# One group of attention and chunk work per slot between the projections of a hybrid decoder layer

## The chip, the cores and the metric

The kernel runs on one core of a Trainium2 chip. The metric is the time of one execution on the device in microseconds. The head loop, which the change touches, is four iterations of the same program.

## The reference, cut to what matters

One layer: a projection of the modulated input h feeds stick-breaking attention (8 heads of 64) and a chunkwise mLSTM (4 heads of 128); both are gated, projected, merged and normed. SEQ and D_MODEL are 1024.

```python
proj = h @ w_in + b_in
...
z = jnp.einsum('bhtd,bhsd->bhts', qb, kb).astype(jnp.float32) * scale
log_beta = jax.nn.log_sigmoid(z)
log_rem = jnp.where(causal, jax.nn.log_sigmoid(-z), 0.0)
suffix = lax.cumsum(log_rem, axis=3, reverse=True) - log_rem
attn = jnp.where(causal, jnp.exp(log_beta + suffix), 0.0)
outs.append(jnp.einsum('bhts,bhsd->bhtd', attn.astype(vb.dtype), vb))
...
qk = jax.nn.silu(causal_depthwise_conv(jnp.concatenate([ml_q, ml_k], -1), conv_w, conv_b))
...
num = (w_inter[..., None] * jnp.einsum('bhtd,bhde->bhte', qb, C)
       + jnp.einsum('bhts,bhse->bhte', s_mat, vb))
...
x = LayerNorm(alpha * x + (1 + gate) * y)
```

## The kernel before, in words

All engines run programs written out by hand; the only order is that of each engine's queue, and semaphores hold them together. Each iteration of the head loop (`iteration`, one per engine) handles one mLSTM head and one pair of attention heads whose q, k, v were projected in the iteration before. Its backbone on TensorE is `project` (L618): nine jobs of 48 matmuls, each 128x128 by 128x512, in which every product is split into three terms (high by high, low by high, high by low). These 432 matmuls are counted through; the number n of a matmul is the clock by which everything else is placed. A job fills two banks (`proj_ps`), one per half of the sequence; ScalarE copies each out behind its 24th matmul (`evac` in `events`, L153) and VectorE and ScalarE split the weights loaded by SP into high and low (`split`). The `tasks` between two values of n are what ScalarE and VectorE do of these.

The attention is cut into NS = 12 slots (`SLOTS`): a block of 128 queries against 1 to 4 blocks of 128 keys (1, 2, 3, 4, 1, 4, 2, 4, 3, 4, 4, 4 blocks). Per slot and for both heads h of the pair: `scores` on TensorE (L716: three products on 64 rows of the array, head 0 in rows 0 to 63, head 1 in rows 64 to 127, into `z_ps[h]`), `odds` on ScalarE (exponential, L998), `cap_odds` on VectorE (L1472), `remainders` on ScalarE (L1007), `stick_left` on VectorE (a scan, L1486), `weights_of` on GpSimd (product, L568), `turn_weights` on TensorE (transposes of the weights back into `z_ps[h]`, L734), `turned` on ScalarE (copy to `at_sb[h]`, L1020) and `weighted_values` on TensorE (L744: 64 columns of the array per head, both heads side by side).

The mLSTM needs a convolution first, over m_k and m_q: `conv_sum` in four halves (L1538, VectorE), `conv_exps` and `conv_sigmoid` on ScalarE with `conv_bound` between them, and `conv_silu` (product, L1556). m_k, v and the mLSTM's v are transposed by `mlstm_third` (L787). From slot 4 on there is one chunk per slot: `mlstm_first` (L763: scores of the chunk, new state, query by state), `chunk_scores` on VectorE (L1578), `mlstm_second` (L780: scores by values), `chunk_values` (L1592); after the last one `norm_head` (L1611).

A slot interrupts the projections twice. At its start TensorE runs `mlstm_first(s)`, `weighted_values(s - 2)` and `scores(s)`; after 13 or 16 projection matmuls it runs `turn_weights(s - 1)`, `mlstm_second(s)` and `mlstm_third(s)`; 14 or 16 more follow. `segments` (L133) has the numbers; `tail` (L147) has those behind slot 11, where the last two slots' values and the last transposes stand alone. ScalarE and VectorE follow the same four marks p0 to p3 of a slot. In this text a slot is one of the twelve, and a group is what TensorE runs between two stretches of projections.

## Time and profile before

| | us |
|---|---|
| median of 3 runs | 979.25 (978.87 to 979.35) |
| profiled execution | 978.75 |
| its span | 977.0 |
| TensorE busy | 942.3 |
| VectorE busy | 599.7 |
| ScalarE busy | 454.5 |
| GpSimd busy | 167.0 |

The mean granted clock of TensorE over the span is 0.997 of full speed. In a timeline the times are microseconds from the span's start; a matmul's length overlaps the next one's, so the distance from start to start is what one costs. A matmul of float32 data (not the split ones) stands as two records, a transpose as one. An entry "x8" is eight records in a row. What stands in brackets is idle time and what ended it.

### The profile page before, as it was taken

Reading aid. Unit: us, or ns where it says so; the run is one execution under the profiler, and the core shown is the slowest. Engines: PE = TensorE matmul, PEld = TensorE weight load, DVE = VectorE, ACT = ScalarE, POOL = GpSimd, SP = SyncE. Lnnn points to the kernel's source line nnn. Section 1 sums busy time; section 2 is a strip of 40 time slices with the busy share of each in tenths; the row PEclk is TensorE's granted clock in tenths of the full one; section 3 lists DMA queues with packets and bytes.
Section 4 is the critical chain, followed back from the end, with each engine's and each line's share of the span. In section 5 each row is a group of like instructions: output and inputs, shape, how many; then the busy total and the mean of one; then the engine's idle time right before and its main releaser. Section 6 shows DMA issues by size and latency. Waiting matters only on the chain.

```text
span 977.0 us, 13097 instructions
## 1 busy us (share of the span) xinstructions
PE 942.3 (96%) x4965; PEld 757.3 (78%) x4965; DVE 599.7 (61%) x1144; ACT 454.5 (47%) x813; POOL 167.0 (17%) x138
## 2 busy tenths in 40 slices
PE   2999999999999999999999999999999999999996
PEld 1677778888778888778888778788888888878885
DVE  4857785666775757866657857543653333345986
ACT  2454575553665544665644756433843222242100
POOL 1010122240132430123220233211100000001200
PEclk9999999999999999999999999999999999999998
DMA  9932211102201012111113101115721222215232
GB/s 231 291 91 55 70 28 44 33 23 69 72 24 54 22 44 85 35 44 34 39 27 98 44 22 45 33 47 189 245 59 43 65 55 52 89 44 182 90 127 86
DMA packets 99561, 73.96 MB, mean 76 GB/s; under 512 B 4616, under 2 KB 90760, under 8 KB 99500
## 3 DMA queue, kind: packets, MB, share of 16 engines
q1 hardware_dynamic: 94828, 58.44, 22.2%
q0 software_dynamic: 2368, 8.41, 2.6%
q10 hardware_dynamic: 2304, 6.29, 1.7%
q8 instruction: 39, 0.64, 0.3%
q14 instruction: 22, 0.18, 0.1%
HBM read 64.59 MB, written 8.40 MB: 75 GB/s over the span
## 4 chain that ended last, share of the span: by engine, by line
PE 82%; DVE 10%; DMA 3%; SPq 2%; ACT 2%; issue 1%; DVEq 0%; ACTq 0%
PE bank L636 41%; PE bank L616 9%; PE bank L615 9%; PE bank L614 9%; PE bank L757 4%; PE bank L741 3%; DMA a_raw<-in_w_ada 2%; PE bank L730 2%; DVE m_q L1547 2%; DVE wL L1344 1%; PE bank L770 1%; SPq L453 1%; DVE m_q L1559 1%; PE bank L713 1%; PE bank L731 1%
## 5 line engine op out<-in xcount | busy, mean ns | idle before, releaser
L636 PE MATMUL bank<-hH,wH 128*128 128x512 f32 x688 | 274.8, 399 | 0.6 <-DVE wL L1344 0.6
L636 PE MATMUL bank<-hL,wH 128*128 128x512 f32 x688 | 272.9, 397 | 0.0
L636 PE MATMUL bank<-hH,wL 128*128 128x512 f32 x688 | 269.1, 391 | 0.0
L574 POOL TENSOR_TENSOR ez<-ez,rem 128x512 f32<-128x512 f32 (+3 forms) x96 | 136.0, 1436 | 411.1 <-DVE rem L1496 411.1
L636 PEld LDWEIGHTS bank<-hH,wH 128*128 128x128 f32 x688 | 129.1, 188 | 38.4 <-issue 10.7
L1344 DVE SCALAR_TENSOR_TENSOR wL<-w_raw,wH 128x512 fp32r<-128x512 f32 x116 | 87.6, 759 | 113.8 <-ACT wH L916 113.3
L636 PEld LDWEIGHTS bank<-hH,wL 128*128 128x128 f32 x688 | 129.4, 188 | 26.6
L636 PEld LDWEIGHTS bank<-hL,wH 128*128 128x128 f32 x688 | 129.4, 188 | 24.6 <-issue 1.0
L916 ACT ACTIVATE wH<-w_raw 128x512 fp32r<-128x512 f32 x116 | 72.5, 627 | 98.0 <-PE bank L616 71.1
L1496 DVE TENSOR_TENSOR_SCAN rem<-rem,ones 128x512 f32<-128x512 f32 (+3 forms) x96 | 88.6, 964 | 38.7 <-ACT rem L1018 38.7
L1005 ACT ACTIVATE ez<-bank 128x512 f32<-128x512 f32 (+3 forms) x96 | 41.9, 489 | 95.1 <-PE bank L732 95.1
L1480 DVE TENSOR_SCALAR ez<-ez 128x512 f32<-128x512 f32 (+3 forms) x80 | 27.5, 344 | 53.7 <-ACT ez L1005 52.7
L614 PE MATMUL bank<-hH,yH 128*128 128x512 f32 x128 | 51.1, 400 | 0.0
L603 POOL TENSOR_TENSOR yL<-yT,yH 128x1024 fp32r<-128x1024 f32 x6 | 14.4, 2398 | 214.5 <-ACT yH L1273 214.5
L616 PE MATMUL bank<-hH,yL 128*128 128x512 f32 x128 | 50.7, 396 | 0.0
L615 PE MATMUL bank<-hL,yH 128*128 128x512 f32 x128 | 50.7, 396 | 0.0
L1014 ACT ACTIVATE rem<-ez 128x512 f32<-128x512 f32 (+3 forms) x96 | 44.9, 517 | 7.2 <-DVE ez L1483 7.1
L1018 ACT ACTIVATE rem<-rem 128x512 f32<-128x512 f32 (+3 forms) x96 | 44.4, 510 | 0.0
L1026 ACT ACTIVATE at<-bank 128x512 f32<-128x512 f32 (+3 forms) x96 | 41.3, 483 | 5.6 <-PE bank L741 5.6
L615 PE MATMUL bank<-hL,wH 128*128 128x512 f32 x112 | 43.7, 390 | 0.0
L614 PE MATMUL bank<-hH,wH 128*128 128x512 f32 x112 | 43.7, 390 | 0.0
L616 PE MATMUL bank<-hH,wL 128*128 128x512 f32 x112 | 43.6, 389 | 0.0
(238 smaller groups left out, 1513.7 us busy)
## 6 DMA issues: line engine op xcount, KB each, us to landing
w_raw<-in_w_in SPq DMA_DIRECT2D x104, 256.0 KB, 2.9
a_raw<-in_w_ada SPq DMA_DIRECT2D x16, 512.0 KB, 7.4
x_rows<-in_x SPq DMA_DIRECT2D x8, 512.0 KB, 6.5
raw<-in_w_ada POOLq DMA_DIRECT2D x8, 512.0 KB, 4.6
x_in<-in_x SPq DMA_DIRECT2D x8, 512.0 KB, 4.2
out_y<-res SPq DMA_DIRECT2D x7, 512.0 KB, 2.9
raw<-in_w_out SPq DMA_DIRECT2D x10, 256.0 KB, 4.8
m_w<-bm_scratch ACTq DMA_DIRECT2D x4, 512.0 KB, 3.9
```

Source lines behind the costliest of these rows:

```text
L574: g.tensor_tensor(e, e, r, ALU.mult).then_inc(a_done[h], 1)
L614: t.matmul(ps, aH, bH, start=k == 0, stop=False)
L615: t.matmul(ps, aH, bL, start=False, stop=False)
L616: return t.matmul(ps, aL, bH, start=False, stop=k == kt - 1)
L636: ins = t.matmul(banks(number)[half][:], w, a, start=(r == 0), stop=(r == JOB_MM // 2 - 1))
L916: a.activation(wH[:, slot, :, 0:width], w_raw[:, slot, :, 0:width], ACT.Copy, scale=scale)\
L1005: a.activation(ez[s % 2][h][:, 0:w], z_ps[h][:, 0:w], ACT.Exp).then_inc(ex_done[h], 1)
L1014: a.activation(rem[s % 2][h][:, 0:w], ez[s % 2][h][:, 0:w], ACT.Ln, bias=1.0).then_inc(ln_done[h], 1)
L1018: a.activation(r, r, ACT.Exp, scale=-1.0).then_inc(rem_done[h], 1)
L1026: a.activation(at_sb[h][:, 0:w], z_ps[h][:, 0:w], ACT.Copy).then_inc(at_out[h], 1)
L1344: v.scalar_tensor_tensor(out=wL[:, slot, :, 0:width], in0=w_raw[:, slot, :, 0:width], scalar=scale, in1=wH[:, slot, :, 0:width], op0=ALU.m ...
L1496: v.tensor_tensor_scan(back, back, ones[:, 0:1].to_broadcast((P, w)), first, ALU.mult, ALU.min)\
```

## The change

On TensorE one group per slot takes the place of the two: group g runs `turn_weights(g - 2)`, `weighted_values(g - 3)`, `mlstm_second(g)` (now for the chunk of slot g - 1), `mlstm_first(g)`, `scores(g)` and `mlstm_third(g)`, then a whole stretch of projections (`GROUPS`: group 0 at n = 48, then 83, 118, 148 and every 26). Groups 12 and 13 hold only what is left over of the turned weights, values and the last chunk; the values of slot 11 stand at the iteration's end. The turned weights of head 0 go to a bank of their own (`misc_ps[2]`), those of head 1 to `z_ps[1]`, ahead of the same group's scores of head 1, which wait for ScalarE's copy of them. `at_sb` has two buffers.

ScalarE copies the turned weights at the start of a slot (`turned(s - 2)`, head 1 first). The convolution's steps stand earlier: the third and fourth sums in slots 0 and 1 (were 1 and 2), the product for m_k in slot 1 (was 2), exponential, bound, sigmoid and product for m_q in slot 2 (were 3). `m_tmp` is made with the chunk's scores; `chunk_values` runs one slot later, ahead of `chunk_scores`, and waits for three fills of its bank. `gate_y(0)` and `store_y(0)` stand one slot later, `norm_head` behind the chunk values of group 12. `place0` to `place2` of ScalarE and VectorE are dissolved into the iterations.

```diff
@@ -130,24 +130,17 @@
-def segments():
-    at, out = PRE, []
-    for s in range(NS):
-        sizes = (8, 8, 16) if s < 3 else (7, 6, 14)
-        row = [at]
-        for n in sizes:
-            at += n
-            row.append(at)
-        out.append(row)
-    return out, JOB_MM * NJ
-def tail():
-    at = segments()[0][-1][-1]
-    return [at, at + (JOB_MM * NJ - at) // 2, JOB_MM * NJ]
+GROUPS = [PRE, 83, 118] + [148 + 26 * n for n in range(NS - 1)]
+JOBS_END = JOB_MM * 9
+def stretch(g):
+    lo, hi = (GROUPS + [JOBS_END])[g:g + 2]
+    return lo, lo + (hi - lo) // 4, lo + (hi - lo) // 2, hi
...
@@ -254,7 +247,7 @@
         rem = [[it(f"rem{b}{h}", [P, HALF]) for h in range(2)] for b in range(2)]
-        at_sb = [it(f"at{h}", [P, HALF]) for h in range(2)]
+        at_sb = [[it(f"at{b}{h}", [P, HALF]) for h in range(2)] for b in range(2)]
         y_stage = it("y_stage", [P, HALF])
...
@@ -390,6 +383,8 @@
             return i * 2 * NJ + (2 * PRO_JOBS + c_)
+        turned_ps = [misc_ps[2], z_ps[1]]
         def banks(number):
...
@@ -718,14 +713,15 @@
                 tt, kk = slice(tb * P, (tb + 1) * P), slice(lo, hi)
+                if s == 0:
+                    pe.wait_ge(pair_split, i * 4 + 4)
                 for h in range(2):
                     r = slice(64 * h, 64 * h + 64)
-                    if s > 1:
-                        pe.wait_ge(at_out[h], i * NS + s - 1)
-                    elif s > 0:
+                    if h and s != 1:
+                        if i or s:
+                            pe.wait_ge(at_out[h], i * NS + max(s - 1, 0))
+                    elif i or s:
                         pe.wait_ge(ex_done[h], i * NS + s)
-                    elif h == 0:
-                        pe.wait_ge(pair_split, i * 4 + 4)
                     ps = z_ps[h][:, 0:hi - lo]
...
@@ -733,12 +729,19 @@
             def turn_weights(i, s):
-                for h in range(2):
-                    if s + 1 < NS:
+                for h in (1, 0):
+                    if h and s < NS - 1:
                         pe.wait_ge(ex_done[h], i * NS + s + 2)
+                    elif h:
+                        pe.wait_ge(at_out[h], i * NS + s)
+                    elif i or s:
+                        pe.wait_ge(at_out[h], i * NS + s)
+                    else:
+                        pe.wait_ge(dec_drained, 1)
                     pe.wait_ge(a_done[h], i * NS + s + 1)
                     for b in range(n_keys(s) // P):
-                        ins = t.transpose(z_ps[h][:, b * P:(b + 1) * P], ez[s % 2][h][:, b * P:(b + 1) * P], ident[:])
+                        ins = t.transpose(turned_ps[h][:, b * P:(b + 1) * P], ez[s % 2][h][:, b * P:(b + 1) * P],
+                                          ident[:])
                     ins.then_inc(at_filled[h], 1)
...
@@ -755,7 +758,7 @@
                         ins = t.matmul(y_ps[64 * h:64 * h + 64, tt], v_tok[:, j, 64 * h:64 * h + 64],
-                                       at_sb[h][:, b * P:(b + 1) * P], start=b == 0 and not continues(s),
+                                       at_sb[s % 2][h][:, b * P:(b + 1) * P], start=b == 0 and not continues(s),
                                        stop=b == n - 1 and closes(s), skip_group_check=True)
...
@@ -766,7 +769,7 @@
                         pe.wait_ge(conv_done, i * 2 + 2)
-                    pe.wait_ge(m_drained[0], m_count(0, i, F_CHUNK + 2 * cc))
+                    pe.wait_ge(m_drained[0], m_count(0, i, F_CHUNK + 2 * cc) - (1 if cc else 0))
                     t.matmul(misc_ps[0][:, 0:P], m_k[:, tt], m_q[:, tt], start=True, stop=True)\
...
@@ -778,8 +781,8 @@
             def mlstm_second(i, s):
-                if s >= 4:
-                    cc = s - 4
+                if s >= 5:
+                    cc = s - 5
                     pe.wait_ge(m_drained[0], m_count(0, i, F_CHUNK + 2 * cc) + 1)
...
@@ -805,25 +808,20 @@
             def iteration(i, last):
-                segs, _ = segments()
                 project(i, 0, PRE)
-                for s in range(NS):
-                    start, _, middle, end = segs[s]
-                    mlstm_first(i, s)
-                    if s > 1:
-                        weighted_values(i, s - 2)
-                    scores(i, s)
-                    project(i, start, middle)
-                    if s > 0:
-                        turn_weights(i, s - 1)
-                    mlstm_second(i, s)
-                    mlstm_third(i, s)
-                    project(i, middle, end)
-                weighted_values(i, NS - 2)
-                ends = tail()
-                project(i, ends[0], ends[1])
-                turn_weights(i, NS - 1)
-                project(i, ends[1], ends[2])
+                for g in range(NS + 2):
+                    if g >= 2:
+                        turn_weights(i, g - 2)
+                    if g >= 3:
+                        weighted_values(i, g - 3)
+                    if g <= NS:
+                        mlstm_second(i, g)
+                    if g < NS:
+                        mlstm_first(i, g)
+                        scores(i, g)
+                        mlstm_third(i, g)
+                    lo, _, _, hi = stretch(g)
+                    project(i, lo, hi)
                 weighted_values(i, NS - 1)
...
@@ -1000,8 +998,6 @@
                     act.wait_ge(z_done[h], i * NS + s + 1)
-                    if s > 1:
-                        act.wait_ge(at_filled[h], i * NS + s - 1)
                     a.activation(ez[s % 2][h][:, 0:w], z_ps[h][:, 0:w], ACT.Exp).then_inc(ex_done[h], 1)
...
@@ -1017,13 +1013,14 @@
                     a.activation(r, r, ACT.Exp, scale=-1.0).then_inc(rem_done[h], 1)
-            def turned(i, s, h):
+            def turned(i, s):
                 w = n_keys(s)
-                act.wait_ge(at_filled[h], i * NS + s + 1)
-                if s > 0:
-                    act.wait_ge(pv_done[h], i * NS + s)
-                a.activation(at_sb[h][:, 0:w], z_ps[h][:, 0:w], ACT.Copy).then_inc(at_out[h], 1)
+                for h in (1, 0):
+                    act.wait_ge(at_filled[h], i * NS + s + 1)
+                    if i * NS + s > 1:
+                        act.wait_ge(pv_done[h], i * NS + s - 1)
+                    a.activation(at_sb[s % 2][h][:, 0:w], turned_ps[h][:, 0:w], ACT.Copy).then_inc(at_out[h], 1)
             def store_y(i, tc):
...
@@ -1137,23 +1130,7 @@
-            def place1(i, s):
...
             def iteration(i, last):
-                segs, _ = segments()
...
@@ -1161,31 +1138,40 @@
                 for s in range(NS):
-                    p0, p1, p2, p3 = segs[s]
+                    p0, p1, p2, p3 = stretch(s)
+                    if s >= 2:
+                        turned(i, s - 2)
                     odds(i, s)
+                    if s == 2:
+                        conv_exps(i, 1)
                     if s == 3:
-                        conv_exps(i, 1)
+                        token_major(i, F_MV, m_vtok)
                     tasks(i, p0, p1, last)
-                    place0(i, s)
                     remainders(i, s)
-                    if s == 3:
+                    if s == 0:
+                        load_forget_row(i)
+                        token_major(i, F_V, v_tok)
+                    if s == 2:
                         conv_sigmoid(i, 1)
+                    if s == 7:
+                        store_y(i, 0)
                     tasks(i, p1, p2, last)
-                    if s > 0:
-                        turned(i, s - 1, 0)
-                        turned(i, s - 1, 1)
-                    place1(i, s)
-                    place2(i, s)
+                    if s == 0:
+                        conv_exps(i, 0)
+                    if s == 2:
+                        act.wait_ge(w_sum, i + 1)
+                        a.activation(m_w[:], m_w[:], ACT.Exp).then_inc(w_exp, 1)
                     tasks(i, p2, p3, last)
-                ends = tail()
-                tasks(i, ends[0], ends[1], last)
-                turned(i, NS - 1, 0)
-                turned(i, NS - 1, 1)
+                    if s == 0:
+                        conv_sigmoid(i, 0)
+                turned(i, NS - 2)
                 act.wait_ge(var_done, i + 1)
                 a.activation(small[:, 24:32], small[:, 16:24], ACT.Ln, bias=EPS).then_inc(rstd_ln, 1)
                 act.wait_ge(rstd_ln, i + 1)
                 a.activation(small[:, 24:32], small[:, 24:32], ACT.Exp, scale=-0.5).then_inc(rstd_exp, 1)
-                tasks(i, ends[1], ends[2], last)
+                tasks(i, GROUPS[NS], GROUPS[NS + 1], last)
+                turned(i, NS - 1)
+                tasks(i, GROUPS[NS + 1], JOBS_END, last)
                 store_y(i, 1)
...
@@ -1584,15 +1570,15 @@
                     .then_inc(m_drained[1], 1)
-            def aggregate(cc):
-                link.mark(v.bn_aggr(mv[:, cc], stat[:, cc]))
-            def chunk_values(i, cc):
-                dve.wait_ge(m_filled[0], m_count(0, i, F_CHUNK + 2 * cc) + 2)
                 v.tensor_scalar(m_tmp[:], misc_ps[1][:, 2 * P:3 * P + 1], h_tok[:, 1, cc:cc + 1], None, ALU.mult)\
                     .then_inc(m_drained[1], 1)
+            def aggregate(cc):
+                link.mark(v.bn_aggr(mv[:, cc], stat[:, cc]))
+            def chunk_values(i, cc):
+                dve.wait_ge(m_filled[0], m_count(0, i, F_CHUNK + 2 * cc) + (2 if cc == NC - 1 else 3))
                 dve.wait_ge(m_drained[1], m_count(1, i, F_CHUNK + 2 * cc) + 2)
...
@@ -1637,28 +1623,7 @@
-            def place0(i, s):
...
             def iteration(i, last):
-                segs, end = segments()
...
@@ -1666,27 +1631,37 @@
                 for s in range(NS):
-                    p0, p1, p2, p3 = segs[s]
-                    place0(i, s)
+                    p0, p1, p2, p3 = stretch(s)
+                    if s >= 5:
+                        chunk_values(i, s - 5)
+                    if s >= 4:
+                        chunk_scores(i, s - 4)
                     cap_odds(i, s)
+                    if s == 1:
+                        conv_silu(i, 0)
                     if s == 2:
-                        conv_silu(i, 0)
-                    if s == 3:
                         conv_bound(i, 1)
-                    if s == 5:
+                    if s == 6:
                         gate_y(i, 0)
                     tasks(i, p0, p1, last)
                     stick_left(i, s)
-                    if s == 3:
+                    tasks(i, p1, p2, last)
+                    if s == 0:
+                        conv_sum(i, 1)
+                        pair_gate(i)
+                        conv_bound(i, 0)
+                    if s == 1:
+                        chunk_weights(i)
+                        conv_sum(i, 3)
+                    if s == 2:
+                        weighted_keys(i)
                         conv_silu(i, 1)
-                    if s >= 4:
-                        chunk_values(i, s - 4)
-                    tasks(i, p1, p2, last)
-                    place1(i, s)
-                    place2(i, s)
                     tasks(i, p2, p3, last)
+                    if s == 0:
+                        conv_sum(i, 2)
+                chunk_values(i, NC - 1)
                 norm_head(i)
-                tasks(i, segs[-1][3], end, last)
+                tasks(i, GROUPS[NS], JOBS_END, last)
                 gate_y(i, 1)
```

## Rows read from the trace of the kernel before

**Rows 1.** The page's part 1, and the longest piece of the chain that ended last.
```profile
PE 942.3 (96%) x4965; PEld 757.3 (78%) x4965; DVE 599.7 (61%) x1144; ACT 454.5 (47%) x813; POOL 167.0 (17%) x138
...
667.12 43.55 PE bank L636 x192
```

**Rows 2.** By line: TensorE's idle time before L713 and L770 (us, times).
```profile
  DVE m_k L1559: 2.5, 4
...
L770 PE MATMUL bank<-m_q,m_k 128*128 128x128 f32 x64 | 12.8, 281 | 2.9 <-DVE m_q L1559 2.9
```

**Rows 3.** Timeline of TensorE, second iteration: start, length (us), what, idle before.
```profile
267.49 0.60 PE L741 MATMUL bank<-ident,ez 128*128 128x128 f32 x4
268.72 1.06 PE L713 MATMUL bank<-ident,m_k 128*128 128x128 f32 x8 [0.63 <-DVE m_k L1559]
...
282.45 0.39 PE L636 MATMUL bank<-hH,wL 128*128 128x512 f32 x1
283.55 0.49 PE L770 MATMUL bank<-m_q,m_k 128*128 128x128 f32 x2 [0.71 <-DVE m_q L1559]
```

**Rows 4.** Timeline of TensorE, slots 4 and 5 of the same iteration.
```profile
288.79 1.03 PE L741 MATMUL bank<-ident,ez 128*128 128x128 f32 x8
289.66 0.39 PE L784 MATMUL bank<-m_vtok,m_s 128*128 128x129 f32 x2
289.81 0.48 PE L636 MATMUL bank<-hL,wH 128*128 128x512 f32 x1
...
293.10 0.38 PE L770 MATMUL bank<-m_q,m_k 128*128 128x128 f32 x2
...
293.54 0.39 PE L777 MATMUL bank<-m_state,m_q 128*128 128x129 f32 x2
293.86 1.09 PE L757 MATMUL bank<-at,v_tok 128*64 128x128 f32 x16
294.88 0.51 PE L730 MATMUL bank<-kH,qH 64*128 64x512 f32 x2
295.22 0.41 PE L731 MATMUL bank<-kL,qH 64*128 64x512 f32 x2
...
295.79 0.50 PE L636 MATMUL bank<-hH,wH 128*128 128x512 f32 x1
```

**Rows 5.** Timeline of TensorE: scores behind projections, transposes behind values.
```profile
254.00 0.39 PE L636 MATMUL bank<-hL,wH 128*128 128x512 f32 x1
254.32 0.39 PE L730 MATMUL bank<-kH,qH 64*128 64x256 f32 x2
...
374.04 1.09 PE L713 MATMUL bank<-ident,m_num 128*128 128x128 f32 x8
374.89 0.47 PE L636 MATMUL bank<-hH,wH 128*128 128x512 f32 x1
```

**Rows 6.** Timeline of VectorE, slots 0 to 2.
```profile
252.11 1.22 DVE L1535 TENSOR_TENSOR g_cur<-next_g,sig 128x1024 f32<-128x1024 f32 x1
...
257.75 1.27 DVE L1496 TENSOR_TENSOR_SCAN rem<-rem,ones 128x256 f32<-128x256 f32 x2 [0.23 <-ACT rem L1018]
...
260.74 0.68 DVE L1554 TENSOR_SCALAR m_num<-m_num 128x1024 f32<-128x1024 f32 x1
...
263.73 0.54 DVE L1545 TENSOR_SCALAR m_q<-conv_in,h_col 128x512 f32<-128x512 f32 x1
...
266.55 0.29 DVE L1480 TENSOR_SCALAR ez<-ez 128x256 f32<-128x256 f32 x1
```

**Rows 7.** Timeline of ScalarE, slots 2 and 3.
```profile
267.07 0.94 ACT L1014 ACTIVATE rem<-ez 128x384 f32<-128x384 f32 x2 [0.50 <-DVE ez L1483]
...
274.06 0.62 ACT L916 ACTIVATE wH<-w_raw 128x512 fp32r<-128x512 f32 x1
...
279.38 1.04 ACT L1119 ACTIVATE sig<-sig 128x1024 f32<-128x1024 f32 x1
...
281.42 0.85 ACT L1026 ACTIVATE at<-bank 128x384 f32<-128x384 f32 x2
```

More of the change, by code:

```diff
@@ L1127, in token_major @@
                                  ACT.Copy).then_inc(m_drained[n], 1)
-            def place0(i, s):
-                if s == 6:
-                    store_y(i, 0)
             def load_forget_row(i):
@@ L1138, in load_forget_row @@
                 act.dma_start(m_w[:].rearrange("p c t -> p (c t)"), row.broadcast_to((P, S))).then_inc(bm_in, 16)
-            def place1(i, s):
-                if s == 0:
-                    load_forget_row(i)
-                    token_major(i, F_V, v_tok)
-            def place2(i, s):
-                if s == 0:
-                    conv_exps(i, 0)
-                if s == 1:
-                    conv_sigmoid(i, 0)
-                    act.wait_ge(w_sum, i + 1)
-                    a.activation(m_w[:], m_w[:], ACT.Exp).then_inc(w_exp, 1)
-                if s == 3:
-                    token_major(i, F_MV, m_vtok)
             def iteration(i, last):
-                segs, _ = segments()
                 act.wait_ge(sig_capped, i * 2 + 1)
@@ L1586, in chunk_scores @@
                     .then_inc(m_drained[1], 1)
+                v.tensor_scalar(m_tmp[:], misc_ps[1][:, 2 * P:3 * P + 1], h_tok[:, 1, cc:cc + 1], None, ALU.mult)\
+                    .then_inc(m_drained[1], 1)
             def aggregate(cc):
@@ L1592, in chunk_values @@
             def chunk_values(i, cc):
-                dve.wait_ge(m_filled[0], m_count(0, i, F_CHUNK + 2 * cc) + 2)
-                v.tensor_scalar(m_tmp[:], misc_ps[1][:, 2 * P:3 * P + 1], h_tok[:, 1, cc:cc + 1], None, ALU.mult)\
-                    .then_inc(m_drained[1], 1)
+                dve.wait_ge(m_filled[0], m_count(0, i, F_CHUNK + 2 * cc) + (2 if cc == NC - 1 else 3))
                 dve.wait_ge(m_drained[1], m_count(1, i, F_CHUNK + 2 * cc) + 2)
@@ L1638, in gate_head @@
                     dve.wait_ge(m_drained[n], m_count(n, i, F_HN) + 1)
-            def place0(i, s):
-                if s >= 4:
-                    chunk_scores(i, s - 4)
-            def place1(i, s):
-                if s == 0:
-                    conv_sum(i, 1)
-                if s == 1:
-                    conv_bound(i, 0)
-            def place2(i, s):
-                if s == 0:
-                    pair_gate(i)
-                if s == 1:
-                    chunk_weights(i)
-                    conv_sum(i, 2)
-                if s == 2:
-                    conv_sum(i, 3)
-                    weighted_keys(i)
             def iteration(i, last):
-                segs, end = segments()
                 split_pair(i)
@@ L1679, in iteration @@
                     stick_left(i, s)
-                    if s == 3:
-                        conv_silu(i, 1)
-                    if s >= 4:
-                        chunk_values(i, s - 4)
-                    tasks(i, p1, p2, last)
-                    place1(i, s)
-                    place2(i, s)
+                    tasks(i, p1, p2, last)
[8 more added lines that the diff above has]
+                        weighted_keys(i)
+                        conv_silu(i, 1)
                     tasks(i, p2, p3, last)
+                    if s == 0:
+                        conv_sum(i, 2)
+                chunk_values(i, NC - 1)
                 norm_head(i)
-                tasks(i, segs[-1][3], end, last)
+                tasks(i, GROUPS[NS], JOBS_END, last)
                 gate_y(i, 1)
```

## The prediction

> **What bounds the kernel now.** The page comes first: TensorE is busy 96% of the span [rows 1]. The other engines matter only where TensorE waits for one of them, or where the change gives TensorE other work or another order. The longest unbroken piece in the chain of waits is 192 projection matmuls in 43.55 us, 0.227 us each [rows 1]; this is the unit below. Next comes the view by line of what TensorE waited for. In the head loop (four iterations) it stops twice per iteration, both times behind the convolution: before the transposes of m_k, 2.5 us in all, four times, and before the first chunk product L770, 2.9 us in all [rows 2]. The timeline gives the whole price. The four transposes at 267.49 need 4 x 0.109 = 0.44 (eight take 289.66 - 288.79 = 0.87 [rows 4]), so the next could start at 267.93 and starts at 268.72: 0.79 lost. The matmul at 282.45 is followed after 1.10, not 0.23: 0.87 lost [rows 3]. That is **1.66 us per iteration, 6.6 us in four**.
>
> **What an interruption costs.** The middle one (transposes, second chunk product): the last chunk product lasts 289.81 - 289.66 = 0.15 where it otherwise takes 0.22, and the 14 projections behind it take 3.29 where 14 x 0.227 = 3.18: net 0.03 to 0.04 us [rows 4]. So stopping the projections for full-array work is nearly free. The other interruption costs more, because its matmuls use half of the array: values are 64 columns wide, scores 64 rows. Entering values adds 0.10 (293.54 to 293.86 is 0.32; two chunk products in front take 0.44, so 0.22 each) [rows 4]. Entering scores from a full-array matmul adds the same: 254.00 to 254.32, 0.32 instead of 0.227 [rows 5]. Leaving values for full-array transposes costs the first transposes: eight of them last 0.85, while 7 x 0.109 plus the 0.03 that remains of a last one before a projection is 0.79: 0.06 more [rows 5]. What counts is changes of shape, not interruptions.
> The Trainium skill (TensorEngine Tiling (Array Packing), Key Properties) says that changing the tiling mode drains the engine. The rows agree, with about 0.1 us each; the page gives no price, and its rule speaks against this change.
>
> **Part by part, per iteration.**
> (a) *Group order on TensorE.* Middle interruptions go: one of V transposes, eleven of turned weights, one in the tail, 13 x 0.03 = -0.4.
> (b) *Shapes.* Before, values pass straight into scores ten times. After, the chunk products stand between them from slot 4 on, and slot 2 has scores without values. Entries into scores from full-array work rise from 2 to 11: +9 x 0.09 = +0.8. Exits from values into full-array work other than a projection rise from 1 to 10: +9 x 0.06 = +0.5. The number of entries into values stays 12. The trace has no chunk product right behind values, so the 0.06 is taken from transposes there; bounds 0 and 0.1. Sum of (b) **+1.3**, bounds +0.8 and +1.8.
> (c) *Convolution moved up.* Both stalls go, -1.66: the product for m_k would end near 258.7, transposes of m_k come near 264.9; the product for m_q ends near 276, the first chunk product comes after 283. What is late next is (d).
> (d) *A new wait between the two heads' scores.* The turned weights of head 1 now go into the bank that head 1's scores of the same group need. ScalarE must copy them out in between. Behind that wait on TensorE stand head 1's scores, transposes and all projections of the stretch. From group 4 on there is cover: from the end of head 1's transposes to the scores lie values, chunk products and head 0's transposes, 1.6 us and more, against two copies of 0.85 in all [rows 7] and an idle ScalarE. Groups 2 and 3 have no chunk products.
> Group 2: TensorE reaches it at 267.49 less ten matmuls (2.3), scores of slot 2 (0.8), values (0.45) and transposes (0.2) = 263.7. Head 1's block is turned at 264.0, copied by 264.25; its scores could start at 264.0. Cost **0.3**.
> Group 3: the copy stands behind all of slot 2 on ScalarE, which in turn waits for VectorE's last convolution sum. VectorE: pair gate until 253.3 [rows 6], then the cap (0.6), sum 2.8, caps of slot 1 0.8, m_k product 1.2, split 0.65, scan 1.2, split 0.65, chunk weights 2.4 and sum 2.85, with a few tenths while GpSimd works beside it: the sum ends at 266.7. (Lengths: 266.55 - 263.73 = 2.82 for a sum; 263.73 - 260.74 = 2.99 for cap and chunk weights; scan 1.27 [rows 6]; the product over 1024 columns as the pair gate, 1.2.) ScalarE from 266.75: exponential 1.0, bias copy 0.6, logarithm and exponential of slot 2 2 x 0.84, the sigmoid's two steps 2.04, split 0.55, exponential of m_w 1.0, bias copy 0.6, split 0.55, head 1's copy 0.35 (281.42 - 279.38 = 2.04; 0.94 for two 384-wide ones that overlap by 0.1; a split 0.62 less the overlap of what follows, a bias copy the same [rows 7]): 8.3, so 275.0. TensorE: 263.7 + 0.2 + scores 1.1 + transposes 0.85 + 30 x 0.227 + 0.1 = 272.7 at group 3; turned weights 0.45 and values 0.45 bring it to 273.6. The six score products of both heads run as pairs, 295.79 - 294.88 = 0.91 [rows 4]. Head 1's start at 275.0 and take the 0.9 alone: cost **1.4**. A VectorE chain faster by 1 us makes it 0.4, one slower by 0.8 makes it 2.2. Sum of (d) **+1.7**, bounds +0.5 and +2.6.
> In program order head 0's three products stand ahead of head 1's. The rows show both first products starting together and then both second ones, 0.34 later [rows 4]. The Trainium skill (TensorE: Matmul & The Clock Gate, Part 3) says matmuls start strictly in program order; by that the second head would start 0.7 later anyhow and (d) would be 0.7 smaller in group 3. The row decides against it.
> (e) *Edits at nothing.* Second buffer for turned weights: its wait is a slot old. m_tmp computed with the chunk scores, chunk values a slot later: VectorE moves 0.3 us of work inside a slot in which it idles. The wait for three fills instead of two holds VectorE's caps behind the first chunk product for some 0.5 us; GpSimd's product has two slots until it is turned, where it had one and a half. The store of y on ScalarE's queue goes one slot later, behind nothing that is needed before the next half. The forget row is issued right after slot 0's remainders, at 248.3 to 248.6 as now, with over 10 us until it is read. SP's loads follow VectorE's splits: the split for matmul 108 is ready near 259.3, needed at 261.4. Head norm: chunk values end some 3.3 us after matmul 382, ScalarE waits for the variance ahead of the bias copy of 384, which ends about 6 us after 382; the bank is wanted at 408, 8 us after. The head's result is wanted 16 us after 382 and is there after 9. Without that cover each microsecond late costs one.
>
> **The sum.** -1.66 - 0.4 + 1.3 + 1.7 = +0.94 per iteration, times 4 = **+3.8 us**. The profiled execution took 978.75 (span 977.0 and 1.75 around it), so 982.5; it stands 0.5 under the median of 979.25, which gives 983.0. I put 982.8.
>
> **Rivals.**
> A, *the new wait is short* (slot 2's chain on ScalarE ends before 274): (d) is 0.6, the sum -0.2 per iteration: 978.5. Against it stands 8.3 us of work on ScalarE that can't start before the last sum. For it, my VectorE chain has ten terms and each may be a tenth too long.
> B, *the shapes cost nothing more and the wait is short*: -1.66 - 0.4 + 0.4 to 0.8 per iteration, 972.5 to 974. For it: no row shows chunk products between values and scores. Against it: entries of 0.1 in every slot, from either kind.
> C, *slower by a lot*: the wait between the heads is unmet in later groups too. It decides where ScalarE is still in its previous tasks when a group begins, by more than the cover of 1.6 us. A bias copy or sigmoid pair due at the end of a stretch (matmul 168 before 174, 384 behind the variance) would do that. Each such slot costs up to 1 us; three per iteration on top of my sum are +12: 995; one is 987. Against it: the last due task lies 6 to 26 matmuls ahead of the group.
> D, *the change doesn't do what it says*, and the chunk product still waits for the convolution: not less than 0.9 per iteration back, 986.4. Seven microseconds of slack speak against it.
>
> **How the numbers follow.** My forecast (981.2 to 986) 0.5; A 0.2; B 0.15; C 0.1; D 0.05. The range takes A, D and the nearer part of both B and C: 976.5 to 987. About 0.2% (2 us) is what a measurement of this kernel can tell from no change. Faster by more than that: B, 0.15 and a little of A, 0.17. Same: most of A and the lower end of the forecast, 0.23. Slower: 0.60.
>
> **What would show it.** In the profile after: no idle time of TensorE before L713 and L770 behind the convolution's product (c); projections interrupted 12 times per iteration with scores and at two more places (a); 0.09 more at each chunk product that leads into scores, with 0.06 at the first behind values (b); in group 3 a gap of 1 to 2 us before head 1's first score product, released by ScalarE's copy of turned weights, and three score products of head 0 alone in front of it (d). If that gap is missing A or B holds. If such gaps are there in groups 4 to 11, C does. A gap before matmul 408 or at the transposes of m_num would say that (e) was wrong about the head norm.

## The result and the profile after

The changed kernel takes **989.0 us** (median, 988.7 to 990.7) against 979.3: a ratio of 1.0105, interval 1.0093 to 1.0117, 9.7 us slower. Forecast were 982.8 us and a range up to 987.0: the direction was right, the size was not. The profiled execution has a span of 987.1 us, 10.1 longer than before.

The page of the changed kernel, part 1 and the engines of the chain that ended last (projections are now L631, values L760, turned weights L743, scores L726 to L728, chunk products L773 to L780 and L787, plain transposes L708):

```profile
span 987.1 us, 13064 instructions
...
PE 954.4 (97%) x4965; PEld 766.4 (78%) x4965; DVE 605.6 (61%) x1144; ACT 456.1 (46%) x813; POOL 165.6 (17%) x138
...
PE 91%; DMA 3%; SPq 2%; DVE 2%; ACT 2%; issue 1%; DVEq 0%; ACTq 0%
```

TensorE is busier than before [rows 1] by 12 us, with the same 4965 records. It makes up 91% of the chain that ended last. Both old stops are gone: no idle time is left before L708 or L773 behind the convolution's product, where the stops had cost 0.79 and 0.87 us per iteration [rows 2, 3]. What came instead stands in group 3. The timeline of TensorE in the second iteration (start, length, what, idle before it):

```profile
274.49 0.60 PE L743 MATMUL bank<-ident,ez 128*128 128x128 f32 x4
275.02 0.44 PE L760 MATMUL bank<-at,v_tok 128*64 128x128 f32 x4
275.39 0.50 PE L726 MATMUL bank<-kH,qH 64*128 64x512 f32 x1
275.73 0.39 PE L727 MATMUL bank<-kL,qH 64*128 64x512 f32 x1
275.96 0.39 PE L728 MATMUL bank<-kH,qL 64*128 64x512 f32 x1
277.39 0.49 PE L726 MATMUL bank<-kH,qH 64*128 64x512 f32 x1 [1.04 <-ACT at L1023]
...
278.28 1.73 PE L708 MATMUL bank<-ident,m_vraw 128*128 128x128 f32 x8
279.66 0.78 PE L631 MATMUL bank<-hL,wH 128*128 128x512 f32 x1
280.23 0.63 PE L631 MATMUL bank<-hH,wL 128*128 128x512 f32 x1
280.66 0.63 PE L631 MATMUL bank<-hH,wH 128*128 128x512 f32 x1
...
282.43 0.39 PE L631 MATMUL bank<-hH,wL 128*128 128x512 f32 x1
282.66 0.40 PE L631 MATMUL bank<-hH,wH 128*128 128x512 f32 x1
```

Head 0's three score products start at 275.39, 275.73 and 275.96. Head 1's first starts only at 277.39, 2.00 us behind head 0's, where both start together in [rows 4]. All four iterations have it; the view of waits (total us, times, longest) names ScalarE's copy of the turned weights for both the weight load and the matmul:

```profile
PEld bank L726 <- ACT at L1023: 5.9, 4, 1.5
...
PE bank L726 <- ACT at L1023: 4.2, 4, 1.1
```

The last lines of the timeline show a second loss. From 280.23 to 280.66 a projection takes 0.43 us; from 282.43 to 282.66 it takes 0.23. The view by stretches gives, for each stretch, the busy time of TensorE, its weight loads, VectorE, ScalarE and GpSimd, then TensorE's granted clock as a share of full speed, the DMA share and GB/s:

```profile
132.20:136.90 4.70, 3.64 (x23) 2.35 (x22) 4.05 (x6) 4.42 (x10) 1.26 (x2) 1.00 0.24 56
274.50:278.60 4.10, 3.06 (x18) 1.83 (x17) 3.54 (x5) 3.82 (x9) 1.17 (x2) 1.00 0.27 63
278.60:282.00 3.40, 3.40 (x14) 2.92 (x12) 1.49 (x5) 2.94 (x6) 0.00 (x0) 0.50 0.30 78
282.00:286.70 4.70, 4.70 (x22) 3.87 (x21) 2.34 (x2) 1.41 (x3) 3.17 (x2) 1.00 0.00 0
...
421.90:425.30 3.40, 3.40 (x14) 2.76 (x13) 2.05 (x6) 2.30 (x6) 0.00 (x0) 0.51 0.46 119
```

From 278.6 to 282.0 the granted clock is 0.50 of full speed, 1.2 GHz instead of 2.4, and again from 421.9. Before each of the two, TensorE had stood idle for 1.04 and 1.05 us; the lower clock began 1.2 and 0.7 us after that idle time ended. The same wait in iterations 1 and 4 (1.06 us each, ending at 135.2 and 565.0) was not followed by it. An iteration lasts 143.84 and 143.77 us in the two that have it, from transposes of m_num to transposes of m_num; it was 140.5.

That two of four iterations have the lower clock belongs to this one execution. Of the four executions of the changed kernel, the slowest (990.7 us) has a mean granted clock of 0.993 and a span 1.7 us longer than the profiled one, as one more such stretch would give. Only one execution was traced, so this is inferred.

Each chunk group from slot 4 on is also longer. Group 5:

```profile
295.46 1.04 PE L743 MATMUL bank<-ident,ez 128*128 128x128 f32 x8
296.43 0.88 PE L760 MATMUL bank<-at,v_tok 128*64 128x128 f32 x12
297.23 0.49 PE L787 MATMUL bank<-m_vtok,m_s 128*128 128x129 f32 x2
297.56 0.39 PE L773 MATMUL bank<-m_q,m_k 128*128 128x128 f32 x2
...
298.00 0.39 PE L780 MATMUL bank<-m_state,m_q 128*128 128x129 f32 x2
298.32 0.51 PE L726 MATMUL bank<-kH,qH 64*128 64x512 f32 x2
```

The first chunk product behind values, L787, takes 297.56 - 297.23 = 0.33 instead of 0.22, and the last one ahead of scores 298.32 - 298.00 = 0.32 instead of 0.22: 0.10 and 0.09 more, in eight groups per iteration.

### The profile page after: what moved, and what is told of

The parts are those of the page before. It is cut to its first block, busy times and chain, and to the rows that moved or that the text cites. A ratio compares the mean times of both kernels' runs of the same rounds, so it can differ in the third digit from the quotient of the medians.

```text
span 987.1 us, 13064 instructions
## 1 busy us (share of the span) xinstructions
PE 954.4 (97%) x4965; PEld 766.4 (78%) x4965; DVE 605.6 (61%) x1144; ACT 456.1 (46%) x813; POOL 165.6 (17%) x138
## 4 chain that ended last, share of the span: by engine, by line
PE 91%; DMA 3%; SPq 2%; DVE 2%; ACT 2%; issue 1%; DVEq 0%; ACTq 0%
PE bank L631 47%; PE bank L611 9%; PE bank L610 9%; PE bank L609 9%; PE bank L760 4%; PE bank L743 3%; DMA a_raw<-in_w_ada 2%; PE bank L726 2%; PE bank L708 2%; PE bank L787 1%; PE bank L727 1%; PE bank L728 1%; SPq L448 1%; PE bank L773 1%; PE bank L778 1%; DVE a_acc L1321 1%
## 5 line engine op out<-in xcount | busy, mean ns | idle before, releaser
L631 PE MATMUL bank<-hH,wH 128*128 128x512 f32 x688 | 271.4, 395 | 0.7 <-DVE wL L1330 0.7
L631 PE MATMUL bank<-hL,wH 128*128 128x512 f32 x688 | 271.0, 394 | 0.0
L631 PE MATMUL bank<-hH,wL 128*128 128x512 f32 x688 | 270.7, 393 | 0.0
L1330 DVE SCALAR_TENSOR_TENSOR wL<-w_raw,wH 128x512 fp32r<-128x512 f32 x116 | 97.7, 844 | 139.0 <-ACT wH L914 138.4
L631 PEld LDWEIGHTS bank<-hH,wH 128*128 128x128 f32 x688 | 129.6, 188 | 31.2 <-issue 3.8
L631 PEld LDWEIGHTS bank<-hH,wL 128*128 128x128 f32 x688 | 129.7, 188 | 30.6 <-issue 3.9
L631 PEld LDWEIGHTS bank<-hL,wH 128*128 128x128 f32 x688 | 129.9, 189 | 27.8 <-issue 1.5
L609 PE MATMUL bank<-hH,wH 128*128 128x512 f32 x112 | 43.7, 390 | 0.0
L760 PE MATMUL bank<-at,v_tok 128*64 128x128 f32 x576 | 42.0, 281 | 0.0
```

What stands on the lines that cost most here:

```text
L609: t.matmul(ps, aH, bH, start=k == 0, stop=False)
L631: ins = t.matmul(banks(number)[half][:], w, a, start=(r == 0), stop=(r == JOB_MM // 2 - 1))
L760: ins = t.matmul(y_ps[64 * h:64 * h + 64, tt], v_tok[:, j, 64 * h:64 * h + 64], at_sb[s % 2][h][:, b * P:(b + 1) * P], start=b == 0 and no ...
L1330: v.scalar_tensor_tensor(out=wL[:, slot, :, 0:width], in0=w_raw[:, slot, :, 0:width], scalar=scale, in1=wH[:, slot, :, 0:width], op0=ALU.m ...
```

## The experiments

After the result the theory was this sum, in us: stalls gone -6.6; head 1 late in group 3, 2.0 x 4 = +8; in group 2, +1.3; the lower clock +3.1; changes of array shape, net of the saved interruptions, +4.1. Together +9.9, against a span longer by 10.1. The 4.1 is what was left when the other terms had been taken off, not a measured term. The rivals: the time is a property of the whole group; ScalarE and VectorE limit slot 2 whatever their order; the clock is a matter of its own. The kernel before, measured beside the experiments, took 978.9 and 979.0 us; every ratio below is against it.

**copy_first** (on the changed kernel; in ScalarE's iteration, and in VectorE's `weighted_keys` ahead of the split of slot 2):

```diff
-                    if s >= 2:
+                    if s >= 2 and s != 3:
                         turned(i, s - 2)
...
                     if s == 2:
-                        act.wait_ge(w_sum, i + 1)
-                        a.activation(m_w[:], m_w[:], ACT.Exp).then_inc(w_exp, 1)
+                        turned(i, 1)
                     tasks(i, p2, p3, last)
+                    if s == 2:
+                        act.wait_ge(w_sum, i + 1)
+                        a.activation(m_w[:], m_w[:], ACT.Exp).then_inc(w_exp, 1)
...
                     stick_left(i, s)
+                    if s == 2:
+                        weighted_keys(i)
                     tasks(i, p1, p2, last)
...
                     if s == 2:
-                        weighted_keys(i)
                         conv_silu(i, 1)
```

> The changed kernel (989.0 us), with ScalarE's copy of the turned weights of slot 1 moved ahead of the bias copy of matmul 144, the split behind it and the exponential of m_w, and VectorE's weighted keys moved ahead of its split in slot 2. Theory (the wait between the two heads' scores in group 3 costs 2.0 us per iteration, and with it come the two stretches at 1.2 GHz, 3.1 us in all): the idle time before head 1's first score product in group 3 goes, the granted clock stays at its upper level through the head loop, and the time falls by 8 + 3 = 11 us to 978. Rival (ScalarE and VectorE are the limit in slot 2, whatever their order): the wait only moves to the transposes behind the scores, the time stays at 985 to 989. Rival on the clock (the two stretches at the lower clock have nothing to do with this wait): they are still there, and the time is 981.

Measured: **977.8 us**, ratio 0.9989 (0.9980 to 0.9998). Group 3 of the second iteration on TensorE:

```profile
273.19 0.50 PE L726 MATMUL bank<-kH,qH 64*128 64x512 f32 x2
...
274.09 1.08 PE L708 MATMUL bank<-ident,m_vraw 128*128 128x128 f32 x8
```

The scores run as pairs again, 0.90 us for six, and the clock stays at its upper level in the whole head loop. The theory's 978 stands; both rivals fall. The span is 11.3 us shorter than the changed kernel's, more than any other part of the change gives or takes. The edit moves ScalarE's copy ahead of three tasks, and moves VectorE's weighted keys along; what each of the two moves gives by itself was not run.

**order** (on the changed kernel) and **both** (order and copy_first together):

```diff
-                    if g >= 3:
-                        weighted_values(i, g - 3)
                     if g <= NS:
                         mlstm_second(i, g)
                     if g < NS:
                         mlstm_first(i, g)
+                    if g >= 3:
+                        weighted_values(i, g - 3)
+                    if g < NS:
                         scores(i, g)
```

> The changed kernel with the chunk's products moved ahead of the values in each group: turned weights, second and first products, values, scores. No work is added or removed. Theory (a change of array shape costs 0.09 us going into scores and 0.10 us coming out of values, 8 groups per iteration): 0.19 x 8 x 4 = 6 us less, 983. Rival (the products cost what they cost, in any order): 989. The wait of group 3 and its stretches at the lower clock stay in both.

> Both edits together on the changed kernel: the copy of slot 1 first, and the chunk's products ahead of the values. Theory: the two gains add, 989 - 11 - 6 = 972; below the kernel before (979.3) by 7. Rival (the copy is then late for the scores in the groups from 4 on, because less TensorE work lies between): 975 to 980.

Measured: order **982.2 us**, ratio 1.0032 (1.0019 to 1.0044); both **971.8 us**, ratio 0.9927 (0.9912 to 0.9942). The gains add. In `order` the idle time of 1.05 to 1.06 us is still there in all four iterations and two of them have the stretch at the lower clock, this time the first and the third. That gives its price: from transposes of m_num to transposes of m_num the second iteration lasts 140.68 us and the third 142.30, with the same wait in both, so one stretch costs 1.6 us. The executions of `order` fall into two groups: three with a mean clock of 0.994 and a span of 981.1 us, three with 0.996 and 979.4 to 979.7, as with one stretch fewer. The median lies between them. The traced executions of `order` and of the changed kernel have two stretches each, and their spans, 981.1 and 987.1, give the price of the order alone: 6.0 us. Group 5 of `both`:

```profile
288.14 1.04 PE L743 MATMUL bank<-ident,ez 128*128 128x128 f32 x8
289.01 0.39 PE L787 MATMUL bank<-m_vtok,m_s 128*128 128x129 f32 x2
289.24 0.39 PE L773 MATMUL bank<-m_q,m_k 128*128 128x128 f32 x2
...
290.00 0.88 PE L760 MATMUL bank<-at,v_tok 128*64 128x128 f32 x12
```

L787 is back at 289.24 - 289.01 = 0.23. With nothing added or removed the order inside the group is worth 6 us. The rival that products cost the same in any order falls.

**conv_only** (on the kernel before; the convolution's steps stand where the change puts them, except that the sigmoid for m_q comes behind the copy of the turned weights of slot 1; excerpt of VectorE and ScalarE):

```diff
                 if s == 0:
                     pair_gate(i)
+                    conv_bound(i, 0)
                 if s == 1:
                     chunk_weights(i)
-                    conv_sum(i, 2)
+                    conv_sum(i, 3)
                 if s == 2:
-                    conv_sum(i, 3)
                     weighted_keys(i)
+                    conv_silu(i, 1)
...
                     tasks(i, p2, p3, last)
+                    if s == 0:
+                        conv_sum(i, 2)
...
-                if s == 1:
-                    conv_sigmoid(i, 0)
+                if s == 2:
+                    conv_sigmoid(i, 1)
                     act.wait_ge(w_sum, i + 1)
```

> The kernel before with only the convolution's steps moved up by a slot, as in the change; two interruptions per slot as before. Theory (the two stalls of 0.79 and 0.87 us per iteration are all that this part of the change can give): 979.3 - 6.6 = 972.7, no idle time before the transposes of m_k and the first chunk product. Rival (moving the steps delays ScalarE's copies of turned weights, and the stall goes to the scores of slot 3): 976 to 980.

Measured: **971.6 us**, ratio 0.9926 (0.9911 to 0.9941). The transposes of m_k follow the turned weights without a pause:

```profile
265.66 0.60 PE L741 MATMUL bank<-ident,ez 128*128 128x128 f32 x4
266.10 1.04 PE L713 MATMUL bank<-ident,m_k 128*128 128x128 f32 x8
```

266.10 - 265.66 = 0.44 is what four transposes take. The span falls by 7.2 us, 0.6 more than the 6.6 that the rows had given. The kernel before shows where it comes from:

```profile
283.88 0.39 PE L775 MATMUL bank<-m_vtok,m_ktok 128*128 128x129 f32 x2
```

The first chunk product, which follows the second stall, starts at 283.55 [rows 3] and takes 283.88 - 283.55 = 0.33, where it takes 0.21 in conv_only without the idle time. The second stall so cost 0.99 us and both together 1.8 per iteration. This part alone, with two interruptions per slot left as they were, is as fast as the best version of the merged group (971.8).

**extra_stop** (on conv_only):

```diff
                         turn_weights(i, s - 1)
-                    mlstm_second(i, s)
                     mlstm_third(i, s)
-                    project(i, middle, end)
+                    project(i, middle, middle + 3)
+                    mlstm_second(i, s)
+                    project(i, middle + 3, end)
```

> The kernel before with the convolution moved up (971.6 us), and one more interruption per slot from slot 4 on: three projection matmuls stand between the turned weights and the chunk's second product. 32 more interruptions of the projections by full-array work. Theory (such an interruption costs 0.03 us): 971.6 + 1.0 = 972.6. Rival (an interruption costs 0.2 us or more, which is what taking one of two per slot away was to bring): 978 or more.

Measured: **972.7 us**, ratio 0.9934 (0.9922 to 0.9946), 1.1 more than conv_only for 32 more interruptions: 0.03 us each, but the intervals of the two overlap. The profiles say the same: the second iteration goes from 138.71 to 138.91 us, 0.03 for each of eight. The rival's 0.2, which would be 6.4 us, is excluded.

**half_wait** (on the changed kernel; `tasks` gets a filter, true for splits alone):

```diff
                         a.activation(m_w[:], m_w[:], ACT.Exp).then_inc(w_exp, 1)
-                    tasks(i, p2, p3, last)
+                        tasks(i, p2, p3, last, False)
+                        turned(i, 1)
+                        tasks(i, p2, p3, last, True)
+                    else:
+                        tasks(i, p2, p3, last)
```

> The changed kernel (989.0 us) with only the split behind matmul 144 moved behind ScalarE's copy of the turned weights of slot 1; exponential and bias copy stay ahead of it. Theory: the idle time before head 1's scores in group 3 falls from 1.05 to about 0.5 us, 0.52 x 4 = 2.1 less. If the stretches at the lower clock come from the length of that idle time they go too, 989 - 2.1 - 3.1 = 983.8; rival (any wait there brings them, or none does): they stay, 986.9.

Measured: **983.9 us**, ratio 1.0050 (1.0036 to 1.0064). Group 3 of the second iteration:

```profile
275.48 0.39 PE L728 MATMUL bank<-kH,qL 64*128 64x512 f32 x1
276.41 0.49 PE L726 MATMUL bank<-kH,qH 64*128 64x512 f32 x1 [0.54 <-ACT at L1023]
```

The idle time is 0.54 us (0.52 to 0.54 in the four iterations), and the granted clock stays at its upper level through the head loop; the mean clock of all four executions is 0.997 or 0.998. Its second iteration lasts 141.72 us where the changed kernel's lasts 143.84: 2.12 less, of which 0.5 is the shorter wait and 1.6 the clock. So the stretches at 1.2 GHz come with this wait at its full length, and half of it doesn't bring them. Why some iterations have them and others with the same wait don't, these runs don't tell.

**between** (on the kernel before, slots 4 to 11):

```diff
-                    mlstm_first(i, s)
                     if s > 1:
                         weighted_values(i, s - 2)
+                    mlstm_first(i, s)
                     scores(i, s)
```

> The kernel before with one swap in each of the slots 4 to 11: values, then the chunk's first three products, then scores (they stood ahead of the values). Nothing is added. Theory (the changes of array shape cost 0.09 + 0.10 us at each of 32 places, whatever else the change does): 979 + 6.2 = 985. Rival (in the changed kernel it was the group as a whole, not the shapes): 979, no difference.

Measured: **981.4 us**, ratio 1.0023 (1.0014 to 1.0032): 2.4 more, neither 6.2 nor nothing. The expectation forgot that in slot 4 the values, 0.8 us, now stand where TensorE had waited 0.87 for the convolution, and hide that stall: its trace has no idle time before L770. 6.2 - 3.5 = 2.7. The shape itself costs what was said:

```profile
294.30 0.49 PE L770 MATMUL bank<-m_q,m_k 128*128 128x128 f32 x2
294.62 0.39 PE L775 MATMUL bank<-m_vtok,m_ktok 128*128 128x129 f32 x2
```

0.32 for the first product behind values, against 0.22: two of them take 293.54 - 293.10 = 0.44 in [rows 4].

**third_early** (on both; the transposes of m_k of group 2 ahead of the scores):

```diff
                         turn_weights(i, g - 2)
+                    if g == 2:
+                        mlstm_third(i, g)
...
                         scores(i, g)
-                        mlstm_third(i, g)
+                        if g != 2:
+                            mlstm_third(i, g)
```

> The changed kernel with the copy of slot 1 first and the chunk's products ahead of the values (971.8 us), and in group 2 the transposes of m_k moved between the turned weights and the scores, 0.85 us of work while ScalarE copies head 1's block. Theory (in group 2 the scores of the two heads run partly one after the other, 0.3 us, and transposes behind scores cost 0.06): 0.38 x 4 = 1.5 less, 970.3. Rival (scores of slot 2 come 0.85 later and ScalarE's chain of slot 2 with them, so that the wait of group 3 comes back): 972 to 974.

Measured: **972.0 us**, ratio 0.9926 (0.9914 to 0.9939): no gain. Groups 2 and 3 of the second iteration:

```profile
262.17 1.03 PE L708 MATMUL bank<-ident,m_k 128*128 128x128 f32 x8
263.14 0.45 PE L726 MATMUL bank<-kH,qH 64*128 64x384 f32 x2
...
271.70 0.74 PE L726 MATMUL bank<-kH,qH 64*128 64x512 f32 x2
272.04 0.39 PE L727 MATMUL bank<-kL,qH 64*128 64x512 f32 x1
...
272.89 1.06 PE L708 MATMUL bank<-ident,m_vraw 128*128 128x128 f32 x8
```

In group 2 the scores run as pairs from 263.14 on, which wins 0.3 us. The transposes ahead of them take 0.97 instead of 0.85, since they now lead into scores. In group 3 the six score products take 272.89 - 271.70 = 1.19 instead of 0.90: head 1 is late again, by 0.3, though without idle time. Won 0.3, lost 0.1 and 0.3: the rival was right in kind.

## Why the prediction was right or wrong

- **(c), the stalls**: right, a little low. Both are gone. They were worth 1.8 us per iteration, not 1.66: conv_only's span is 7.2 shorter, because the first product behind a stall is slower too.
- **(a), an interruption costs 0.03**: right (extra_stop). The middle interruptions were nearly free; at this price taking them away gives about 1.5 us in all (an estimate: the second iteration's projections are broken 27 times before and 15 after, 12 fewer, where the sum had 13).
- **(b), shapes**: right in kind, a little low. Entering scores +0.09 as forecast; leaving values +0.10 to 0.11 instead of 0.06. That term was read from plain transposes behind values; a chunk product behind values pays more. The net of (a) and (b) was forecast at 3.6 us. It was not measured by itself; copy_first's span leaves 975.8 - 977.0 + 7.2 - 1.3 = 4.7 for it (7.2 for the stalls, 1.3 for group 2). The prices found here would give 9 x 0.09 + 9 x 0.10 - 12 x 0.03 = 1.35 per iteration, 5.4 us; the difference of 0.7 stays open.
The Trainium skill (TensorEngine Tiling (Array Packing), Key Properties) says that a change of tiling mode drains the engine. The runs between, order and both agree with it: each change costs about 0.1 us.
- **(d), head 1's wait**: right in mechanism and place, but 0.6 us too short in group 3, 2.4 us in four iterations. Group 2 cost 0.32, as said; its timeline shows head 1's first product 0.33 behind head 0's:

```profile
265.68 0.44 PE L726 MATMUL bank<-kH,qH 64*128 64x384 f32 x1
265.96 0.34 PE L727 MATMUL bank<-kL,qH 64*128 64x384 f32 x1
266.01 0.44 PE L726 MATMUL bank<-kH,qH 64*128 64x384 f32 x1
266.14 0.33 PE L728 MATMUL bank<-kH,qL 64*128 64x384 f32 x1
...
266.73 1.09 PE L708 MATMUL bank<-ident,m_k 128*128 128x128 f32 x8
```

Group 3 cost 2.0 where the sum had 1.4 and its bound 2.2. ScalarE, second iteration:

```profile
269.18 1.06 ACT L1111 ACTIVATE sig<-m_q 128x1024 f32<-128x1024 f32 x1 [1.80 <-DVE m_q L1535]
...
274.94 1.04 ACT L1163 ACTIVATE m_w<-m_w 128x1024 f32<-128x1024 f32 x1
275.88 0.67 ACT L955 ACTIVATE m_vraw<-bank,h_col 128x512 f32<-128x512 f32 x1
276.45 0.61 ACT L914 ACTIVATE wH<-w_raw 128x512 fp32r<-128x512 f32 x1
276.97 0.64 ACT L1023 ACTIVATE at<-bank 128x256 f32<-128x256 f32 x2
```

From the exponential for m_q at 269.18 to the start of the copy it is 7.8 us, and head 1's scores could start 8.2 after it, against 8.3 in the sum. So ScalarE's part was right. What was late was its start, which VectorE feeds:

```profile
262.23 1.16 DVE L1330 SCALAR_TENSOR_TENSOR wL<-w_raw,wH 128x512 fp32r<-128x512 f32 x1
263.31 1.75 DVE L1552 TENSOR_TENSOR m_w<-m_w,h_tok 128x1024 f32<-128x1024 f32 x1
...
266.25 0.54 DVE L1531 TENSOR_SCALAR m_q<-conv_in,h_col 128x512 f32<-128x512 f32 x1
```

The split at 262.23 takes 1.16 and the first step of the chunk weights 1.75, where 0.69 and 1.21 stand elsewhere; GpSimd multiplies from 261.8 to 264.0. The rest of the trace agrees: from 90 to 680 us, 52 splits of this shape overlap no GpSimd product and take 0.68 or 0.69 us, 24 overlap one and take 1.15 to 1.76. "A few tenths while GpSimd works beside it" was 1.0. The sum of slot 1 ends at 269.1. The forecast's times lie 1.8 us earlier (it has the pair gate end at 253.3, the trace at 255.1), so that is 267.3 in its terms instead of 266.7: all of the 0.6.
- **The step that failed** is the price of the wait in (d). The sum charged it by its length alone, at its bound too (2.2 us), and put the granted clock at nothing without a reason. The forecast cost of 1.4 us was only partly idle time: head 1's start at 275.0 less head 0's at 273.6 and 0.9 of products leaves 0.4 to 0.5 us of idle TensorE. Near that length the price was right: half_wait has a cost of 1.5 us with 0.54 of it idle, the clock stays up, and its 983.9 lies inside the range. The cost of 2.0 that came instead has 1.04 to 1.06 us of idle time. Half of those waits in the profiled execution were followed by 3.4 us at half the clock, 1.6 us lost each time, 3.2 in all. No row before could give this price, since the longest idle time in the head loop was 0.72 us; a wait longer than any in the rows should not have been priced from them. So the mis-sized VectorE chain, which lengthened the wait, cost 2.4 us, and the clock, which had no term, 3.2 more. Without the latter the time would be 985.8, inside the range; with it, it is not. The bounds of (b) and (d) added up give 988.4, above the stated end of 987 and still under the 989.0 measured.
- **(e)**: right. Nothing waits at matmul 408 or at the transposes of m_num.
- **Rivals**: A (short wait) and B fell here. copy_first, which takes the wait of group 3 away, took 977.8 where A had 978.5. C asked for waits in later groups; there is none. D fell, since no chunk product waits for the convolution.

In sums: -7.2 for stalls, +4.7 for shapes and interruptions, +9.3 for waits between the heads, +3.2 for the clock: 10.0, with a span longer by 10.1. The 4.7 is what copy_first leaves over, and the other terms are read from traces.

## What to carry to other kernels

Count changes of array shape, not interruptions: a stop of the main stream for full-array work cost 0.03 us, each change between full, half-column and half-row tiles about 0.1, and keeping the full-array products together in front of the tiled ones gave 6 us at no cost. Where a copy is put between two matmuls of the same group, follow its engine's queue back to the last thing it waits for, and take out of the way what is not yet needed: here, a copy moved ahead of three tasks was 11 us, 3 of them for the clock. Price a wait of TensorE longer than any in the rows with a possible fall of the granted clock. Before merging groups, try the moved-up dependency alone; here it was the whole gain (971.6), and the merged group, mended twice (971.8), only came level with it.

## What the runs showed of the hardware that was not expected

- An idle time of TensorE of 1.04 to 1.06 us between dense work was followed, in two of four places in the profiled execution of each of two kernels, by 3.4 us at a granted clock of 0.5, which cost 1.6 us. It began 0.7 to 1.4 us after the idle time ended. An idle time of 0.52 to 0.54 us was not followed by it in four places (half_wait), nor were those of 0.62 to 0.72 in the kernel before.
- Leaving 64-column values costs a following chunk product 0.10 to 0.11 us, a plain transpose 0.06. A chunk product behind an idle TensorE took 0.33 instead of 0.21.
- A 128x512 split on VectorE took 1.16 instead of 0.69 us and a 128x1024 addition 1.75 instead of 1.21 while GpSimd multiplied.
- Score products on the two halves of the array's rows start in pairs although one head's stand ahead of the other's in the program. In group 2 head 1's first product starts at 266.01, before head 0's third at 266.14. When the second head waits they run one after the other, 1.7 us of products instead of 0.9.
